# A heads stage whose next head begins in the tail of the current one, with the gate projected ahead of the values

## The chip, the cores and the metric

One Trainium2 chip, one core of it. The metric is device time in microseconds of the whole program. The program runs several stages one behind the other; the change touches one of them, the stage of heads, which takes the stretch from about 125 to 1003 us of a profiled execution of 5142.65 us.

## What is computed

The stage computes, for each of 8 heads of 128 channels, a bidirectional gated linear recurrence over 512 tokens that starts from the state of 256 context tokens, and one block of a depthwise convolution with 31 taps. Cut to what matters here:

```python
f = lb + (1 - lb) * sigmoid(z);  log_f = log(f);  k = (1 - lb) * sigmoid(-z)   # per direction
S_t = diag(f_t) S_{t-1} + k_t outer v_t;   o_t = S_t^T q_t                    # forward and backward
q = silu(x @ w_q);  v = x @ w_i;  gate = silu(x @ w_g)
hg = rms_norm(o_f + o_b) * silu(gate)
u = a * sigmoid(g)                                                            # conv_glu
u = depthwise_conv(u, 31 taps) + bias
```

Everything is float32, the matrix products too. Each head needs nine projections: `ca` and `cg` (the two inputs of the convolution), the gate logits of the two directions, the same two for the context, `q`, the values `v` for the 512 tokens, the values for the context, and `gate`.

## The kernel before

`phase_heads` runs one loop over the 8 heads on each engine, with the engines tied by counting semaphores. Nothing orders the work but the order in which each engine's program is written.

- **SyncE** loads the seven weight tiles of a head (512 KB each) into a ring of 7 slots, each as soon as its slot is free.
- **TensorE** calls `fill(n, head)` for the nine projections, n = 0 to 8. Fills 6, 7 and 8 of a head open the body of that head. Then come nine levels of a divide-and-conquer: for the first seven, two score products each (L734, on `qk`), and behind level 1 to 6 one of the fills 0 to 5 of the *next* head. Then the rest of the scores (L744, L749, L755, L761, L772), the output product with the values (L779, L781) and the sum of squares (L785).
- **VectorE** makes the logarithms and `k` from what ScalarE left (L890 to L895), and then runs the levels: three taps of the convolution, two running sums (L941, L950), the product `qk` (L966), and two masked copies out of PSUM (`to_blocks`, L928). After level 8 come the last taps, `ksum` (L973), `full` (L976, L977) and the last masked copy. The body ends with the scaling by the reciprocal root (L982) and the product with the gate (L985).
- **ScalarE** copies the projections out of PSUM (`evacuate`), computes the exponentials that each level needs (`grow`, L840), and has a tail: copies of the scores (L850 to L861), copy and square of the output (L864, L865), then `gates` of the next head (three copies, Abs, Exp, Ln: L809 to L818), the reciprocal root of this head (L869, L871) and `queries` of the next head (Silu).

A "tap" is one `scalar_tensor_tensor` on 128x512, 31 for each head. Of a fill, TensorE can start only when the bank it writes was copied out; a fill n below 4 waits for all nine copies of the head before. "Tail" below is the stretch from the start of the last masked copy of a head (level 8 is over) to the first running sum of the next head.

Of the kernel before, what the change touches and what calls it, by code (L numbers as in the profile page):

```python
# [12 lines left out]
ALU = mybir.AluOpType  # L13
# [585 lines left out]
def phase_heads(nc, io, mem):  # L599
# [20 lines left out]
    LINKS_DVE = 2 + 2 * LEVELS  # L620
    with Phase(nc, "hd") as ph:

        w = ph.stream(RING, [(1, AHEAD, [0, 1, 4, 4, 5]), (HEADS - 1, F, [1, 2, 3, 4, 7, 7, 8]),
                             (1, F - AHEAD, [1, 2])])
# [36 lines left out]
        @block.sync  # L661
        def _(sp):
            def load(t, head):
                load_tile(sp, w, *place(t, head), io["w_head"][head, t])
# [12 lines left out]
        def _(pe):  # L677
# [20 lines left out]
            def fill(n, head):  # L698
# [3 lines left out]
                if n < 4:  # L702
                    last = project(n, head, mem.xmT, bank)
                elif n == 4:
                    project(2, head, mem.cmT, bank[:, 0:C])
                    last = project(3, head, mem.cmT, bank[:, C:2 * C])
                elif n == 5:
                    last = project(4, head, mem.xmT, bank)
                elif n == 6:
                    last = tokens(5, head, mem.xmT, TB, bank)  # L710
                elif n == 7:
                    last = tokens(5, head, mem.cmT, CB, bank)
                else:
                    last = project(6, head, mem.xmT, bank)
                last.then_inc(w.filled, 1)

            def body(i, more):
# [59 lines left out]
                pe.wait_ge(proj_out, START + i * F + 8)  # L777
# [16 lines left out]
        def _(act):  # L794
# [10 lines left out]
            def gates(head):  # L805
# [10 lines left out]
                nc.scalar.activation(pre[:], pre[:], ACT.Exp, scale=-1.0).then_inc(act_seq, 1)  # L816
                act.wait_ge(act_seq, START + head * 2 + 2)
                nc.scalar.activation(pre[:], pre[:], ACT.Ln, bias=mem.c("one")).then_inc(ln_ready, 1)  # L818

            def queries(head):  # L820
                evacuate(5, head, q[:], B[1], ACT.Silu)

            def body(i, more):
                act.wait_ge(lk_ready, START + i + 1)
                nc.scalar.activation(k[:], k[:], ACT.Exp).then_inc(k_ready, 1)
                act.wait_ge(o_filled, START + i)
                evacuate(6, i, v[:, 0:TB, :], B[2].rearrange("p (b n) -> p b n", b=TB))
                evacuate(7, i, v[:, TB:TB + CB, :], B[3][:, 0:C].rearrange("p (b n) -> p b n", b=CB))
                act.wait_ge(head_done, START + i)
                evacuate(8, i, gate[:], B[0], ACT.Silu)  # L830
                for level in range(LEVELS):
# [34 lines left out]
                if more:  # L866
                    gates(i + 1)
# [4 lines left out]
                if more:  # L872
                    queries(i + 1)

            conv_inputs(0)
            gates(0)
            queries(0)
# [5 lines left out]
        def _(dve):  # L883
# [3 lines left out]
            with dve.Fori(0, HEADS) as i:  # L887
                seq.body(i, LINKS_DVE)
                dve.wait_ge(ln_ready, START + i + 1)
# [3 lines left out]
                nc.vector.memset(suf[:], 0.0)  # L893
# [3 lines left out]

                dve.wait_ge(proj_out, START + i * F + 2)
                dve.wait_ge(tapped, START + i * TAPS)
                nc.vector.tensor_tensor(out=upad[:, TAPS // 2:TAPS // 2 + T], in0=ca[:], in1=cg[:],  # L900
                                        op=ALU.mult).then_inc(conv_read, 1)
                weights = mem.p("dw").rearrange("p (b k) -> p b k", b=DB)[:, i, :]
                acc = mem.convT[:, i, :]
                left = list(range(TAPS))

                def taps(n):

                    for _ in range(min(n, len(left))):
                        tap = left.pop(0)
                        if tap == 0:  # L910
                            dve.wait_ge(conv_read, START + i + 1)
                            ins = nc.vector.tensor_scalar(acc, upad[:, 0:T], weights[:, 0:1],
                                                          mem.p("conv_b")[:, bass.ds(i, 1)], ALU.mult, ALU.add)
                        else:
                            dve.wait_ge(tapped, START + i * TAPS + tap)
                            ins = nc.vector.scalar_tensor_tensor(out=acc, in0=upad[:, tap:tap + T],
                                                                 scalar=weights[:, tap:tap + 1], in1=acc,
                                                                 op0=ALU.mult, op1=ALU.add)
                        ins.then_inc(tapped, 1)
# [52 lines left out]
                taps(TAPS)  # L972
# [6 lines left out]
                to_blocks(N_MASKS - 1)  # L979

# [5 lines left out]
            seq.end(HEADS)  # L986
# [2128 lines left out]
```

## Time and profile before

| what | value |
|---|---|
| median of three runs | 5145.26 us (5143.11 to 5145.98) |
| profiled execution, its own time | 5142.65 us |
| its span | 5140.9 us |
| mean granted clock of TensorE | 0.949 of full speed |
| busy over the span: TensorE, VectorE, ScalarE | 89%, 54%, 34% |
| stage of heads | about 125 to 1003 us |

A time stamp in the trace is microseconds from the start of the span. The shares are averages over stages that are limited by different engines; for this change only the stretch of the heads counts. A granted clock of 1.0 is 2.4 GHz, of 0.5 it is 1.2 GHz.

### The profile page before, as it was taken

Reading aid. Unit: us, or ns where it says so; the run is one execution under the profiler, and the core shown is the slowest. Engines: PE = TensorE matmul, PEld = TensorE weight load, DVE = VectorE, ACT = ScalarE, POOL = GpSimd, SP = SyncE. Lnnn points to the kernel's source line nnn. Section 1 sums busy time; section 2 is a strip of 40 time slices with the busy share of each in tenths; the row PEclk is TensorE's granted clock in tenths of the full one; section 3 lists DMA queues with packets and bytes.
Section 4 is the critical chain, followed back from the end, with each engine's and each line's share of the span. In section 5 each row is a group of like instructions: output and inputs, shape, how many; then the busy total and the mean of one; then the engine's idle time right before and its main releaser. Section 6 shows DMA issues by size and latency. Waiting matters only on the chain. (4 is left out here: it accounts for less than half of the span.)

```text
span 5140.9 us, 60695 instructions
## 1 busy us (share of the span) xinstructions
PE 4583.3 (89%) x21819; PEld 3657.5 (71%) x21819; DVE 2766.2 (54%) x5003; ACT 1741.5 (34%) x2490; POOL 412.8 (8%) x308
## 2 busy tenths in 40 slices
PE   7988888588899856699999999698999999999998
PEld 5555555344587425699999999576778877678787
DVE  0557775522334599788888887434343333444332
ACT  0243333223432103333333332336432233452322
POOL 0000000000000160122222222000000000000000
PEclk8999999799999979899999999899999999999999
DMA  6100110000122102678777875221222321113222
GB/s 259 58 29 29 37 37 21 21 28 16 41 94 93 49 19 123 228 274 282 272 274 276 280 274 200 70 70 44 73 92 96 95 86 62 50 62 98 89 95 84
DMA packets 195766, 575.47 MB, mean 112 GB/s; under 512 B 17312, under 2 KB 66720, under 8 KB 194336
## 3 DMA queue, kind: packets, MB, share of 16 engines
q1 hardware_dynamic: 157888, 433.77, 24.4%
q0 software_dynamic: 36864, 134.23, 7.7%
q10 hardware_dynamic: 864, 5.45, 0.3%
q8 instruction: 95, 1.56, 0.1%
q14 instruction: 55, 0.45, 0.0%
HBM read 546.13 MB, written 27.26 MB: 112 GB/s over the span
## 5 line engine op out<-in xcount | busy, mean ns | idle before, releaser
L402 DVE TENSOR_TENSOR tile_rest<-tile_raw,tile_up 128x1024 fp32r<-128x1024 f32 (+2 forms) x288 | 338.7, 1181 | 781.0 <-ACT tile_up L393 780.9
L410 PE MATMUL layer_psum<-hn_up,tile_up 128*128 128x512 f32 x1344 | 534.7, 398 | 21.2 <-DVE hn_rest L497 21.2
L411 PE MATMUL layer_psum<-hn_up,tile_rest 128*128 128x512 f32 x1344 | 527.0, 392 | 0.0
L412 PE MATMUL layer_psum<-hn_rest,tile_up 128*128 128x512 f32 x1344 | 526.7, 392 | 0.0
L393 ACT ACTIVATE tile_up<-tile_raw 128x1024 fp32r<-128x1024 f32 (+2 forms) x288 | 291.4, 1017 | 368.8 <-PE layer_psum L412 368.4
L687 PE MATMUL hd_psum<-xmT,hd_w 128*128 128x512 f32 x768 | 341.5, 599 | 15.7 <-DMA hd_w<-in_w_head 15.7
L1896 PE MATMUL ex_psum<-ex_t_up,ex_u_up 128*128 128x384 f32 x1024 | 344.2, 336 | 10.7 <-ACT ex_prod L1970 6.3
L1914 PE MATMUL ex_psum<-ex_prod_up,ex_v_up 128*128 128x384 f32 x1024 | 342.8, 335 | 3.8 <-DVE xT L2036 3.8
L1897 PE MATMUL ex_psum<-ex_t_up,ex_u_rest 128*128 128x384 f32 x1024 | 343.9, 336 | 0.0
L1898 PE MATMUL ex_psum<-ex_t_rest,ex_u_up 128*128 128x384 f32 x1024 | 343.7, 336 | 0.0
L1915 PE MATMUL ex_psum<-ex_prod_up,ex_v_rest 128*128 128x384 f32 x1024 | 342.6, 335 | 0.0
L1916 PE MATMUL ex_psum<-ex_prod_rest,ex_v_up 128*128 128x384 f32 x1024 | 342.6, 335 | 0.0
L410 PEld LDWEIGHTS layer_psum<-hn_up,tile_up 128*128 128x128 f32 x1344 | 255.2, 190 | 81.7 <-issue 29.7
L411 PEld LDWEIGHTS layer_psum<-hn_up,tile_rest 128*128 128x128 f32 x1344 | 255.1, 190 | 53.9 <-issue 1.9
L412 PEld LDWEIGHTS layer_psum<-hn_rest,tile_up 128*128 128x128 f32 x1344 | 254.7, 189 | 53.9
L687 PEld LDWEIGHTS hd_psum<-xmT,hd_w 128*128 128x128 f32 x768 | 144.6, 193 | 180.6 <-issue 180.6
L1962 ACT ACTIVATE ex_v_up<-tT 128x1024 fp32r<-128x1024 f32 x128 | 128.7, 1052 | 305.4 <-PE ex_psum L1916 301.7
L734 PE MATMUL hd_psum<-hd_qk 128*128 128x128 f32 x896 | 139.0, 320 | 91.3 <-DVE hd_qk L966 91.3
L734 PEld LDWEIGHTS hd_psum<-hd_qk 128*128 128x128 f32 x896 | 133.4, 232 | 115.2 <-issue 68.1
L1896 PEld LDWEIGHTS ex_psum<-ex_t_up,ex_u_up 128*128 128x128 f32 x1024 | 193.7, 189 | 11.4 <-issue 11.4
L1914 PEld LDWEIGHTS ex_psum<-ex_prod_up,ex_v_up 128*128 128x128 f32 x1024 | 192.7, 188 | 4.2 <-DVE xT L2036 4.2
L2036 DVE SCALAR_TENSOR_TENSOR xT<-ex_psum,modulation,xT 128x384 f32<-128x384 f32 x256 | 156.8, 612 | 71.7 <-PE ex_psum L1916 71.7
(415 smaller groups left out, 9532.8 us busy)
## 6 DMA issues: line engine op xcount, KB each, us to landing
ex_u<-in_peer_u SPq DMA_DIRECT2D x128, 512.0 KB, 6.7
tT<-in_peer_v SPq DMA_DIRECT2D x128, 512.0 KB, 7.2
tile_raw<-in_w_gu SPq DMA_DIRECT2D x88, 512.0 KB, 3.3
hd_w<-in_w_head SPq DMA_DIRECT2D x56, 512.0 KB, 3.9
mod_w<-in_w_ada SPq DMA_DIRECT2D x48, 512.0 KB, 4.9
mg_w_raw<-in_w_merge SPq DMA_DIRECT2D x48, 512.0 KB, 3.3
expert_table<-et_rows SPq DMA_DIRECT2D x6, 4096.0 KB, 11.7
ex_rows<-expert_table SPq DMA_DIRECT2D x64, 384.0 KB, 7.9
```

What stands on the lines that cost most here:

```text
L393: self.nc.scalar.activation(self.up[:, n % self.SLOTS, 0:blocks, :], self.raw[n % self.RAWS][:, 0:blocks, :], ACT.Copy).then_inc(self.up_r ...
L402: self.nc.vector.tensor_tensor(out=self.rest[:, n % self.SLOTS, 0:blocks, :], in0=self.raw[n % self.RAWS][:, 0:blocks, :], in1=self.up[:, ...
L410: self.nc.tensor.matmul(dst, w_up, up, start=first, stop=False)
L411: self.nc.tensor.matmul(dst, w_rest, up, start=False, stop=False)
L412: return self.nc.tensor.matmul(dst, w_up, rest, start=False, stop=last)
L687: last = nc.tensor.matmul(dst, weights[:, d, :], rhs[:, d, :], start=d == 0, stop=d == DB - 1)
L1896: nc.tensor.matmul(dst, u_up[par, t][:, d, :], t_up[:, d, :], start=d == 0, stop=False)
L1897: nc.tensor.matmul(dst, u_rest[par, t][:, d, :], t_up[:, d, :], start=False, stop=False)
L1898: last = nc.tensor.matmul(dst, u_up[par, t][:, d, :], t_rest[:, d, :], start=False, stop=d == DB - 1)
L1914: nc.tensor.matmul(dst, v_up[par, t][:, m, :], prod_up[par, t][:], start=first, stop=False)
L1915: nc.tensor.matmul(dst, v_rest[par, t][:, m, :], prod_up[par, t][:], start=False, stop=False)
L1916: last = nc.tensor.matmul(dst, v_up[par, t][:, m, :], prod_rest[par, t][:], start=False, stop=final)
```

## The change

Six edits, all in the stage of heads.

1. VectorE: a new function `start(head)` holds the opening of a head (clearing `suf`, the product `upad`, taps 0 to 13, the logarithms and `k`). It is called for head 0 ahead of the loop, and for head i+1 in the body of head i, between the last masked copy and the scaling by the reciprocal root.
2. VectorE: the levels then do 2 taps each instead of 3; level 8 does the one that is left. None stands behind level 8.
3. The body of the last head is written out behind the loop on VectorE, as it already was on TensorE and ScalarE.
4. ScalarE: `gates` is split. `decays` (three copies, Abs, Exp) stands ahead of the copy of the output, `log_decays` (Ln) where `gates` stood.
5. ScalarE: the copy of `q` moves out of the tail into the opening of the body, behind the exponential of `k`; `gate` follows it; the two copies of the values move behind `grow` of level 1.
6. TensorE: fill 6 is now the gate, fills 7 and 8 the values; the weight tiles are loaded in that order too. The output product waits for all nine copies.

The diff, cut to its core:

```diff
+    EARLY_TAPS = 14
-        w = ph.stream(RING, [(1, AHEAD, [0, 1, 4, 4, 5]), (HEADS - 1, F, [1, 2, 3, 4, 7, 7, 8]),
-                             (1, F - AHEAD, [1, 2])])
+        w = ph.stream(RING, [(1, AHEAD, [0, 1, 4, 4, 5]), (HEADS - 1, F, [0, 2, 3, 4, 7, 7, 8]),
+                             (1, F - AHEAD, [0, 2])])
...
                 elif n == 6:
-                    last = tokens(5, head, mem.xmT, TB, bank)
+                    last = project(5, head, mem.xmT, bank)
                 elif n == 7:
-                    last = tokens(5, head, mem.cmT, CB, bank)
+                    last = tokens(6, head, mem.xmT, TB, bank)
                 else:
-                    last = project(6, head, mem.xmT, bank)
+                    last = tokens(6, head, mem.cmT, CB, bank)
...
             def body(i, more):
                 act.wait_ge(lk_ready, START + i + 1)
                 nc.scalar.activation(k[:], k[:], ACT.Exp).then_inc(k_ready, 1)
-                act.wait_ge(o_filled, START + i)
-                evacuate(6, i, v[:, 0:TB, :], B[2].rearrange("p (b n) -> p b n", b=TB))
-                evacuate(7, i, v[:, TB:TB + CB, :], B[3][:, 0:C].rearrange("p (b n) -> p b n", b=CB))
+                evacuate(5, i, q[:], B[1], ACT.Silu)
                 act.wait_ge(head_done, START + i)
-                evacuate(8, i, gate[:], B[0], ACT.Silu)
+                evacuate(6, i, gate[:], B[2], ACT.Silu)
...
+                    if level == 1:
+                        act.wait_ge(o_filled, START + i)
+                        evacuate(7, i, v[:, 0:TB, :], B[3].rearrange("p (b n) -> p b n", b=TB))
+                        evacuate(8, i, v[:, TB:TB + CB, :], B[0][:, 0:C].rearrange("p (b n) -> p b n", b=CB))
...
+                if more:
+                    decays(i + 1)
                 act.wait_ge(masked, START + i * N_MASKS + N_MASKS)
                 act.wait_ge(o_filled, START + i + 1)
...
                 if more:
-                    gates(i + 1)
+                    log_decays(i + 1)
...
-                if more:
-                    queries(i + 1)
...
+            def start(head):
+
+                nc.vector.memset(suf[:], 0.0)
+                dve.wait_ge(proj_out, START + head * F + 2)
+                dve.wait_ge(tapped, START + head * TAPS)
+                nc.vector.tensor_tensor(out=upad[:, TAPS // 2:TAPS // 2 + T], in0=ca[:], in1=cg[:],
+                                        op=ALU.mult).then_inc(conv_read, 1)
+                taps(head, 0, EARLY_TAPS)
+                dve.wait_ge(ln_ready, START + head + 1)
                 seq(nc.vector.scalar_tensor_tensor(out=pre[:], in0=k[:], scalar=0.0, in1=pre[:], op0=ALU.min,
                                                    op1=ALU.subtract))
                 nc.vector.tensor_sub(k[:], pre[:], k[:]).then_inc(lk_ready, 1)
...
-                    taps(3)
+                    taps(i, EARLY_TAPS + 2 * level, EARLY_TAPS + 2 * level + 2)
...
                 to_blocks(N_MASKS - 1)
+                if more:
+                    start(i + 1)
 
                 dve.wait_ge(rstd_ready, START + i + 1)
```

VectorE at the end of a head, before (`hd_o` is the scaled output, `hgT` the head's result); what stands behind the last row here is the head of the loop, with L890 first:

```order
L977 TENSOR_TENSOR hd_full<-hd_full,hd_q 128x2x512
L925 REGISTER_ALU
L928 COPY_PREDICATED hd_sx<-masks,hd_psum 128x4x128
L982 SCALAR_TENSOR_TENSOR hd_o<-hd_o,params,hd_orstd 128x512
```

and the same place of the change, where 14 taps write `convT` between the masked copy and `hd_o`:

```order
L979 TENSOR_TENSOR hd_full<-hd_full,hd_q 128x2x512
L927 REGISTER_ALU
L930 COPY_PREDICATED hd_sx<-masks,hd_psum 128x4x128
L908 MEMSET hd_suf 128x1536
L909 ISA
L910 ISA
L911 TENSOR_TENSOR hd_upad<-hd_conv_a,hd_conv_g 128x512
...
L915 SCALAR_TENSOR_TENSOR hd_pre<-hd_k,hd_pre 128x1536
L221 REGISTER_ALU
L917 TENSOR_TENSOR hd_k<-hd_pre,hd_k 128x1536
L919 TENSOR_SCALAR hd_pre<-hd_pre 128x1536
L986 SCALAR_TENSOR_TENSOR hd_o<-hd_o,params,hd_orstd 128x512
```

The whole opening of the next head has moved ahead of `hd_o` and of the wait for `hd_orstd` in front of it.

ScalarE in the tail, before (`hd_sc` are scores of the context, `hd_osq` the squared output, `hd_pre` the logarithms being made):

```order
L861 ACTIVATE hd_sc<-hd_psum 128x512
L862 ISA
L864 ACTIVATE hd_o<-hd_psum 128x512
L865 ACTIVATE hd_osq<-hd_psum 128x512
...
L814 ACTIVATE hd_pre<-hd_k 128x1536
L815 ISA
L816 ACTIVATE hd_pre<-hd_pre 128x1536
L817 REGISTER_ALU
L818 ACT_TABLE_LOAD
L818 ACTIVATE hd_pre<-hd_pre,consts 128x1536
L869 ACTIVATE hd_orstd<-hd_psum,consts 128x512
```

and of the change:

```order
L863 ACTIVATE hd_sc<-hd_psum 128x512
L808 ISA
L809 ISA
...
L815 ACTIVATE hd_pre<-hd_k 128x1536
L816 ISA
L817 ACTIVATE hd_pre<-hd_pre 128x1536
L866 ISA
L868 ACTIVATE hd_o<-hd_psum 128x512
L869 ACTIVATE hd_osq<-hd_psum 128x512
L820 REGISTER_ALU
L821 ACT_TABLE_LOAD
L821 ACTIVATE hd_pre<-hd_pre,consts 128x1536
L873 ACTIVATE hd_orstd<-hd_psum,consts 128x512
```

The three copies, Abs and Exp now stand ahead of the copy of the output; Ln still stands between the square and the reciprocal root. At the head of ScalarE's loop the change has:

```order
L825 ACT_TABLE_LOAD
L825 ACTIVATE hd_k<-hd_k 128x1536
L798 ISA
L799 ACT_TABLE_LOAD
L799 ACTIVATE hd_q<-hd_psum 128x512
L827 REGISTER_ALU
L798 REGISTER_ALU
L799 ACTIVATE hd_gate<-hd_psum 128x512
L830 ISA
L838 ACT_TABLE_LOAD
L838 ACTIVATE hd_grow<-hd_suf 128x256
```

Before, the two copies of the values and a table load of their own for `hd_gate` stood in the place of `hd_q` and its load.

## Rows read from the trace of the kernel before

**Rows 1.** Stretch, length, busy PE PEld DVE ACT POOL, PE's granted clock, DMA share, GB/s.

```profile
497.00:512.00 15.00, 6.39 (x32) 6.21 (x33) 12.73 (x25) 5.40 (x13) 0.00 (x0) 0.69 0.00 0
512.00:565.00 53.00, 50.91 (x194) 30.32 (x192) 47.02 (x92) 13.23 (x30) 0.00 (x0) 0.99 0.13 46
```

**Rows 2.** Who waited for whom, 280 to 1003 us: us in total, times, longest.

```profile
DVE hd_o L982 <- ACT hd_orstd L871: 182.3, 8, 23.9
```

**Rows 3.** VectorE's timeline, one tail: start, length, instruction, idle before and releaser.

```profile
463.30 0.73 DVE L928 COPY_PREDICATED hd_sx<-masks,hd_psum 128x512 f32<-128x512 uint8 x1 [0.30 <-PE hd_psum L744]
487.50 0.75 DVE L982 SCALAR_TENSOR_TENSOR hd_o<-hd_o,params,hd_orstd 128x512 f32<-128x512 f32 x1 [23.47 <-ACT hd_orstd L871]
...
489.07 1.75 DVE L890 SCALAR_TENSOR_TENSOR hd_pre<-hd_k,hd_pre 128x1536 f32<-128x1536 f32 x1
...
492.88 1.34 DVE L893 MEMSET hd_suf<- 128x1536 f32 x1 [0.27 <-issue]
...
499.75 1.03 DVE L941 TENSOR_TENSOR hd_suf<-hd_suf,hd_pre 128x384 f32<-128x384 f32 x2 [1.47 <-ACT hd_grow L840]
```

**Rows 4.** VectorE's timeline, levels of the head that follows.

```profile
510.40 2.53 DVE L916 SCALAR_TENSOR_TENSOR convT<-hd_upad,params,convT 128x512 f32 x3
512.85 1.02 DVE L941 TENSOR_TENSOR hd_suf<-hd_suf,hd_pre 128x384 f32<-128x384 f32 x2
...
565.50 0.68 DVE L973 TENSOR_TENSOR hd_ksum<-hd_k 128x512 f32<-128x512 f32 x1
```

**Rows 5.** ScalarE's timeline, the same tail.

```profile
476.48 0.60 ACT L864 ACTIVATE hd_o<-hd_psum 128x512 f32<-128x512 f32 x1 [5.57 <-PE hd_psum L781]
...
477.45 1.58 ACT L798 ACTIVATE hd_k<-hd_psum 128x512 f32<-128x512 f32 x3
...
482.08 1.28 ACT L818 ACT_TABLE_LOAD   x1
483.37 1.57 ACT L818 ACTIVATE hd_pre<-hd_pre,consts 128x1536 f32<-128x1536 f32 x1
...
492.65 1.48 ACT L825 ACTIVATE hd_k<-hd_k 128x1536 f32<-128x1536 f32 x1 [1.97 <-DVE hd_k L892]
...
498.27 0.43 ACT L840 ACTIVATE hd_grow<-hd_suf 128x256 f32<-128x256 f32 x1
```

**Rows 6.** TensorE's timeline, the same tail.

```profile
461.40 1.66 PE L744 MATMUL hd_psum<-hd_q,hd_ksum 128*128 128x128 f32 x8 [3.42 <-DVE hd_ksum L973]
...
466.68 3.60 PE L772 MATMUL hd_psum<-hd_full 128*128 128x512 f32 x8
...
478.57 7.31 PE L694 MATMUL hd_psum<-hd_w,xmT 128*128 128x128 f32 x64
...
489.29 7.03 PE L687 MATMUL hd_psum<-xmT,hd_w 128*128 128x512 f32 x16
```

**Rows 7.** TensorE's timeline, levels 1 and up of the head that follows.

```profile
509.04 3.25 PE L734 MATMUL hd_psum<-hd_qk 128*128 128x128 f32 x16 [2.29 <-DVE hd_qk L966]
...
519.44 1.95 PE L734 MATMUL hd_psum<-hd_qk 128*128 128x128 f32 x16
521.23 7.03 PE L687 MATMUL hd_psum<-xmT,hd_w 128*128 128x512 f32 x16
528.09 1.95 PE L734 MATMUL hd_psum<-hd_qk 128*128 128x128 f32 x16
```

**Rows 8.** VectorE's waits for TensorE at levels 6 and 7 of that head.

```profile
546.70 0.73 DVE L928 COPY_PREDICATED hd_sx<-masks,hd_psum 128x512 f32<-128x512 uint8 x1 [1.15 <-PE hd_psum L734]
...
555.39 0.73 DVE L928 COPY_PREDICATED hd_sx<-masks,hd_psum 128x512 f32<-128x512 uint8 x1 [1.31 <-PE hd_psum L734]
```

**Rows 9.** Head 0: TensorE's first fill 6; VectorE's scaling of heads 0 and 6.

```profile
165.70 7.31 PE L694 MATMUL hd_psum<-hd_w,xmT 128*128 128x128 f32 x64
...
279.27 0.75 DVE L982 SCALAR_TENSOR_TENSOR hd_o<-hd_o,params,hd_orstd 128x512 f32<-128x512 f32 x1 [23.49 <-ACT hd_orstd L871]
...
903.92 0.75 DVE L982 SCALAR_TENSOR_TENSOR hd_o<-hd_o,params,hd_orstd 128x512 f32<-128x512 f32 x1 [23.47 <-ACT hd_orstd L871]
```

More of the change, by code:

```diff
@@ L663, in load @@
             def load(t, head):
-                load_tile(sp, w, *place(t, head), io["w_head"][head, t])
+                load_tile(sp, w, *place(t, head), io["w_head"][head, (0, 1, 2, 3, 4, 6, 5)[t]])
             for t in range(5):
@@ L803, in conv_inputs, with decays @@
                 evacuate(1, head, cg[:], B[1], ACT.Sigmoid)
-            def gates(head):
+            def decays(head):
                 act.wait_ge(qk_ready, START + head * (LEVELS + 2))
@@ L871, in body @@
                 nc.scalar.activation(orstd[:], orstd[:], ACT.Exp, scale=-0.5).then_inc(rstd_ready, 1)
-                if more:
-                    queries(i + 1)
             conv_inputs(0)
-            gates(0)
-            queries(0)
+            decays(0)
+            log_decays(0)
             with act.Fori(0, HEADS - 1) as i:
@@ L886, in _, with taps @@
             seq = Order(dve, dve_seq)
-            with dve.Fori(0, HEADS) as i:
-                seq.body(i, LINKS_DVE)
-                dve.wait_ge(ln_ready, START + i + 1)
+            def taps(head, first, past):
+                weights = mem.p("dw").rearrange("p (b k) -> p b k", b=DB)[:, head, :]
+                acc = mem.convT[:, head, :]
+                for tap in range(first, min(past, TAPS)):
+                    if tap == 0:
+                        dve.wait_ge(conv_read, START + head + 1)
+                        bias = mem.p("conv_b")[:, bass.ds(head, 1)]
+                        ins = nc.vector.tensor_scalar(acc, upad[:, 0:T], weights[:, 0:1], bias, ALU.mult, ALU.add)
+                    else:
+                        dve.wait_ge(tapped, START + head * TAPS + tap)
+                        ins = nc.vector.scalar_tensor_tensor(out=acc, in0=upad[:, tap:tap + T],
+                                                             scalar=weights[:, tap:tap + 1], in1=acc,
+                                                             op0=ALU.mult, op1=ALU.add)
+                    ins.then_inc(tapped, 1)
+            def start(head):
[6 more added lines that the diff above has]
+                dve.wait_ge(ln_ready, START + head + 1)
                 seq(nc.vector.scalar_tensor_tensor(out=pre[:], in0=k[:], scalar=0.0, in1=pre[:], op0=ALU.min,
@@ L892, in _, with body @@
                 nc.vector.tensor_sub(k[:], pre[:], k[:]).then_inc(lk_ready, 1)
-                nc.vector.memset(suf[:], 0.0)
                 nc.vector.tensor_scalar_max(pre[:], pre[:], LN_TINY).then_inc(logs_ready, 1)
[L898 to L919, printed above, removed]
+            def body(i, more):
                 def to_blocks(n):
@@ L971, in _ @@
                         to_blocks(2 * level - 1)
-                taps(TAPS)
+                taps(i, EARLY_TAPS + 2 * LEVELS, TAPS)
                 nc.vector.tensor_tensor(out=ksum[:], in0=k[:, 0, 0:T], in1=k[:, 1, 0:T],
@@ L985, in _ @@
                 nc.vector.tensor_tensor(out=mem.hgT[:, i, :], in0=o[:], in1=gate[:], op=ALU.mult).then_inc(head_done, 1)
-            seq.end(HEADS)
+            seq.body(0, 1)
+            start(0)
+            seq.end(1)
+            with dve.Fori(0, HEADS - 1) as i:
+                seq.body(i, LINKS_DVE)
+                body(i, True)
+            seq.end(HEADS - 1)
+            seq.body(0, LINKS_DVE - 1)
+            body(HEADS - 1, False)
+            seq.end(1)
             dve.wait_ge(head_done, START + HEADS)
```

5 lines of the change are left out of this document (2 added, 3 removed).

## The prediction, made before the change was run

> **What bounds the kernel now.** I first read who waited for whom in the stage of heads. One wait stands out: VectorE waits 182.3 us over 8 heads for `hd_orstd` before it scales the output, 23 us in each head [rows 2]. Then I read the timelines of the three engines through one such tail. VectorE ends level 8 with the masked copy at 463.30 and does nothing until 487.50 [rows 3]. ScalarE meanwhile copies the output at 476.48, then does the next head's three copies, Abs, Exp and Ln (477.45 to 484.9), and only then the reciprocal root [rows 5]. After the wait VectorE opens the next head: logarithms at 489.07, clearing at 492.88, first running sum at 499.75 [rows 3]. All this is work of the next head that needs nothing of this head's output.
>
> Next I looked at what TensorE does, for it has a limit of its own. It ends a head's last fill at 458, waits 3.42 for `ksum`, finishes the output sum at 478.57 and projects fills 6 to 8 from there [rows 6]. From level 1 on it repeats one pattern: a score pair and a fill, 519.44 to 528.09, 8.65 us [rows 7]. VectorE's level takes 7.28, of which three taps are 510.40 to 512.85, 2.45 us, 0.82 a tap [rows 4]. So TensorE is already the slower of the two in the levels, and VectorE waits for it 1.15 us at level 6 and 1.31 at level 7 [rows 8]. In levels 1 to 8 TensorE is busy 50.9 of 53 us [rows 1]. What VectorE gains beyond these waits is therefore not all gained by the head. A head now takes (903.92 - 279.27) / 6 = 104.1 us [rows 9].
>
> **The change part by part.** I follow one steady head and call F the start of fill 6, 478.57 [rows 6].
>
> *ScalarE's tail.* The three copies, Abs and Exp take 482.08 - 477.45 = 4.63 [rows 5] and move ahead of the output copy. There ScalarE idles 5.57 [rows 5], so they cost nothing, with 0.9 to spare. If that cover were gone, each microsecond of lateness would delay the output copy and with it L785 and F. The table load and Ln, and with them the reciprocal root, come earlier by 4.5: Ln starts at 483.37 - 4.5 = 478.85 (F+0.3), `ln_ready` is at F+1.85, and the root is ready at F+4.4 instead of F+8.93 [rows 3, 5].
>
> *VectorE's tail.* The opening now follows the masked copy. From 492.88 to 499.75, less the wait of 1.47, a clearing, L895, `upad` and three taps take 5.40 [rows 3]. Eleven more taps are 9.0, the copy and the issue gap 0.9: together 15.3 from the start of the masked copy. That copy starts 1 us behind L744, and `ln_ready` is 17.3 us behind L744 (below, 15.47 + 1.85). So 14 taps, 11.5 us a head, lie in idle time, and VectorE still waits 2 us for Ln. Then L915 and L917 take 492.88 - 489.07 - 0.27 = 3.54 [rows 3], so `lk_ready` comes at F+5.4. L919 (0.81), the scaling and the product with the gate (489.07 - 487.50 = 1.57 [rows 3]) end by F+8. Queued behind them are two taps and the first running sum.
>
> *ScalarE's opening.* Behind the root the loop's table load ends at F+5.7, a little after `lk_ready`. Then come Exp of `k`, a load, `q`, `gate` and a load. Before, the stretch from Exp of `k` to the first `grow` was 498.27 - 492.65 = 5.62 [rows 5], with the copies of the values and a short wait in it; now it has `q` instead of these, 5.3. I take `grow` at F+11.0, and VectorE's first running sum 1.48 later [rows 3, 5], at F+12.45 instead of F+21.18: 8.7 us earlier.
>
> *TensorE.* Fills 6 to 8 are the same work in another order: 10.72 for the values (489.29 - 478.57) [rows 6] and 8.65 - 1.79 = 6.86 for the gate [rows 7], 17.58 in all, ending at F+17.6. The gate is ready at F+7, before it is asked for (F+8). Level 0's `qk` is ready at F+15.9, so the 7 us idle ahead of level 0 are gone. Level 0's scores end at F+19.4. Level 1's `qk` comes at 509.04 - 8.7 - 0.82 (one tap less), F+20.95, so TensorE waits 1.5 there [rows 7]. Then six patterns of 8.65 follow, 51.9, and the last fill ends at F+72.85. VectorE's `ksum` is ready earlier: before, it started 65.75 after the first running sum (565.50 - 499.75) [rows 3, 4]; less 13 taps (10.7) and the waits of 2.46 [rows 8] it starts at F+65.1. So VectorE is ahead and waits inside the levels, some 7 us in all. From L744 to the next F it is 478.57 - 461.40 = 17.17 now [rows 6], of which the first 5.28 (461.40 to 466.68) hold 4,096 columns at the lower clock, right behind 3.42 idle. 2,048 columns take 1.79 in [rows 7] at the full clock, so 3.58 without the idle, and L744 to F is 15.47. Period: 72.85 + 15.47 = **88.3 us**, 15.8 less than 104.1.
>
> *The late copies of the values.* They wait on ScalarE for fill 8 (F+17.6), behind `grow` of level 1; `grow` of level 2 is queued behind them. TensorE needs the ninth copy for fill 0 at F+22.7, VectorE needs `grow` of level 2 at F+24. Both have 4 us to spare. *The tiles* are asked for in the new order almost a head ahead, and the DMA share is 0.13 [rows 1]: nothing. *The written-out body* adds no work.
>
> *Sum.* Head 0: F is 165.70 [rows 9], its scaling falls at 165.70 + 88.3 + 6.3 = 260.3 instead of 279.27: 19.0. Six periods of 15.8: 94.8. The last head has no fills, so there VectorE's own path counts: from scaling to first running sum 6.3 less (12.25 [rows 3] to 5.95), and 13 taps less, 10.7: 17.0. Together 130.8 us. The profiled execution took 5142.65, so 5011.9; the median of the runs is 2.6 higher, and I forecast **5014**.
>
> *A rule against it.* ScalarE's path to level 0 has five table loads behind the output copy. In this trace Ln starts 1.29 us after its load does and the load is 1.28 long, with no gap ahead of it either [rows 5]: a load costs 1.28. The Trainium skill, page "ScalarE: Activation LUTs", section "What ACT_TABLE_LOAD costs", puts a drain of some 1.38 us on top of each switch. By that page level 0 would be some 6.9 us later, TensorE's wait at level 1 as much longer, and the time an estimated 48 us more, 5062. The rows have no such gap, and I go by the rows.
>
> **The rivals.**
>
> *TensorE keeps falling to the lower clock (5050).* In 497 to 512 the granted clock is 0.69, behind 7 us of idle, and a score stretch takes 3.25 instead of 1.95 [rows 1, 7]. If the remaining waits (1.5 at level 1, some 2 in the tail) had the same effect, levels 0 and 1 would cost 3.4 more and L744 to F 1.7 more: 5.1 in each of 7 heads, 36 us. Against it: behind the 0.7 and 1.2 of the present tail, fills run at full speed (10.72 for the values [rows 6]).
>
> *VectorE's own path sets the period (4965).* If TensorE's waits vanished from the levels, the head would follow VectorE, 7 us less, 49 us in all. Against it stand the 8.65 of [rows 7], which nothing in the change shortens.
>
> *The tail work lands on the path (no change).* If the early three copies waited for something late, ScalarE would reach the output copy late, and the 14 taps would push the scaling. It takes a lateness of 15.8 us a head to eat the gain; I see at most 0.9 us missing.
>
> *Slower: fills at half clock.* A fill is 6.86 at 2.4 GHz and 13.7 at 1.2. The gain of 15.8 is gone once 2.3 of a head's nine fills run at the lower level; with four of nine there it is 7 x (27.4 - 15.8) = 81 us slower, 5226. It would need short gaps to bring the clock down. The stretch with most fills has 0.99 [rows 1].
>
> **How the numbers follow.** The forecast as walked has 0.66, its own range 5000 to 5030: without TensorE's wait at level 1 it is 10 us lower, with 2 us a head more it is 14 higher. The lower clock (5050) has 0.17, the drain 0.02, a smaller unforeseen wait between these and 5100 has 0.04, VectorE's path 0.04, no change 0.03, slower 0.04. The range 4998 to 5052 takes in the first two. What a measurement of this kernel can tell from no change is 0.2%, 10 us: faster 0.93, same 0.03, slower 0.04.
>
> **What would show it.** Right: VectorE's wait for the reciprocal root is gone, 2 us before L915 in its place; the scalings of heads 0 and 6 are 530 us apart; VectorE waits for TensorE's scores from level 4 on, and TensorE's patterns stay at 8.65; the granted clock in the heads is above 0.97; `qk` of level 0 finds TensorE still in fill 8. Wrong: TensorE idle ahead of level 0, the output copy later than 5.6 us behind the last score copy, score stretches of 3 us in the loop, or taps slower than 0.82 while ScalarE works on `k`.

## The result, and the profile of the changed kernel

The changed kernel takes a median of **5011.89 us** (5008.62 to 5017.14, four runs); the kernel before took 5145.62 on the same chip (5143.11 to 5149.23, four runs). The ratio is 0.9741, with a 95% interval of 0.9724 to 0.9757: 133.7 us less. The forecast was 5014.

The page of the changed kernel opens with its span, and its first group gives busy time, share and instructions of each engine. VectorE, with 2767.6 us of busy time, does what it did; what shrank are the span and TensorE's busy time (4583.3 before), which is shorter where the clock is up.

```profile
span 5012.3 us, 60591 instructions
...
PE 4546.6 (91%) x21819; PEld 3631.0 (72%) x21819; DVE 2767.6 (55%) x5003; ACT 1730.1 (35%) x2481; POOL 412.9 (8%) x308
```

The view of waits, for 250 to 890 us (us in total, times, longest), answers to [rows 2]: the 182.3 us that VectorE waited for the reciprocal root are gone in all heads but the last, where no next head is there to be opened. In their place VectorE now waits for TensorE's scores, at most 2.2 us at a time.

```profile
DVE hd_sx L930 <- PE hd_psum L735: 36.6, 18, 2.2
...
DVE hd_o L986 <- ACT hd_orstd L875: 17.5, 1, 17.5
```

VectorE's timeline (start, length, instruction, idle before and releaser) answers to [rows 3, 4, 8, 9]. 261.25 and 791.38 are the scalings of heads 0 and 6, 869.15 that of the last head. From 417.54 on it is one tail: masked copy, clearing, 13 taps in one row, then the logarithms at 433.63 with a wait of 0.74 for Ln, and the first running sum at 444.14. The rows at 479.88 to 497.23 are waits for the scores of levels 4 to 6, which VectorE copies in its own levels 5 to 7, as [rows 8] counts them.

```profile
261.25 0.74 DVE L986 SCALAR_TENSOR_TENSOR hd_o<-hd_o,params,hd_orstd 128x512 f32<-128x512 f32 x1
...
417.54 0.73 DVE L930 COPY_PREDICATED hd_sx<-masks,hd_psum 128x512 f32<-128x512 uint8 x1 [1.25 <-PE hd_psum L745]
...
418.52 1.34 DVE L908 MEMSET hd_suf<- 128x1536 f32 x1 [0.25 <-issue]
...
421.39 11.50 DVE L901 SCALAR_TENSOR_TENSOR convT<-hd_upad,params,convT 128x512 f32 x13
433.63 1.76 DVE L915 SCALAR_TENSOR_TENSOR hd_pre<-hd_k,hd_pre 128x1536 f32<-128x1536 f32 x1 [0.74 <-ACT hd_pre L821]
...
444.14 1.03 DVE L943 TENSOR_TENSOR hd_suf<-hd_suf,hd_pre 128x384 f32<-128x384 f32 x2 [2.96 <-ACT hd_grow L838]
...
479.88 0.73 DVE L930 COPY_PREDICATED hd_sx<-masks,hd_psum 128x512 f32<-128x512 uint8 x1 [1.85 <-PE hd_psum L735]
...
488.53 0.73 DVE L930 COPY_PREDICATED hd_sx<-masks,hd_psum 128x512 f32<-128x512 uint8 x1 [2.04 <-PE hd_psum L735]
...
497.23 0.73 DVE L930 COPY_PREDICATED hd_sx<-masks,hd_psum 128x512 f32<-128x512 uint8 x1 [2.19 <-PE hd_psum L735]
...
791.38 0.75 DVE L986 SCALAR_TENSOR_TENSOR hd_o<-hd_o,params,hd_orstd 128x512 f32<-128x512 f32 x1
...
869.15 0.75 DVE L986 SCALAR_TENSOR_TENSOR hd_o<-hd_o,params,hd_orstd 128x512 f32<-128x512 f32 x1 [17.47 <-ACT hd_orstd L875]
```

ScalarE's timeline of the same tail answers to [rows 5]. The idle time ahead of the output copy is 1.14 us instead of 5.57, for three copies, Abs and Exp now stand ahead of it. The table load at 430.73 follows it, and Ln 1.29 behind the load's start.

```profile
429.62 0.60 ACT L868 ACTIVATE hd_o<-hd_psum 128x512 f32<-128x512 f32 x1 [1.14 <-PE hd_psum L782]
...
430.73 1.28 ACT L821 ACT_TABLE_LOAD   x1
432.02 1.57 ACT L821 ACTIVATE hd_pre<-hd_pre,consts 128x1536 f32<-128x1536 f32 x1
```

TensorE's timeline answers to [rows 6, 7]. Fill 6 starts at 431.72, level 0's scores at 449.31 right behind fill 8, level 1's at 452.53 behind a wait of 1.27. From there to the next L745, at 504.59, nothing waits.

```profile
416.24 1.05 PE L745 MATMUL hd_psum<-hd_q,hd_ksum 128*128 128x128 f32 x8
...
430.76 1.13 PE L786 MATMUL hd_psum<-hd_osq,consts 128*128 128x512 f32 x2 [1.23 <-ACT hd_osq L869]
431.72 7.03 PE L688 MATMUL hd_psum<-xmT,hd_w 128*128 128x512 f32 x16
...
449.31 1.95 PE L735 MATMUL hd_psum<-hd_qk 128*128 128x128 f32 x16
452.53 2.05 PE L735 MATMUL hd_psum<-hd_qk 128*128 128x128 f32 x16 [1.27 <-DVE hd_qk L968]
454.41 7.03 PE L688 MATMUL hd_psum<-xmT,hd_w 128*128 128x512 f32 x16
...
504.59 1.05 PE L745 MATMUL hd_psum<-hd_q,hd_ksum 128*128 128x128 f32 x8
```

The windows of the changed kernel (columns as in [rows 1]): TensorE is busy for 40.00 of 40 us in the levels, VectorE for 32.23, and the granted clock is 1.00 there and 0.97 over the stage.

```profile
464.00:504.00 40.00, 40.00 (x158) 24.75 (x157) 32.23 (x66) 11.90 (x26) 0.00 (x0) 1.00 0.12 42
...
125.00:870.00 745.00, 692.89 (x3055) 448.50 (x3053) 573.37 (x1023) 310.64 (x560) 0.00 (x0) 0.97 0.11 38
```

The period of a head is (791.38 - 261.25) / 6 = **88.36 us**, 15.75 less than the 104.11 of before.

### The profile page after: what moved, and what is told of

Its sections match the earlier page's. It is cut to its first block and busy times, and to the rows that moved or that the text cites. A ratio compares the mean times of both kernels' runs of the same rounds, so it can differ in the third digit from the quotient of the medians.

```text
span 5012.3 us, 60591 instructions
## 1 busy us (share of the span) xinstructions
PE 4546.6 (91%) x21819; PEld 3631.0 (72%) x21819; DVE 2767.6 (55%) x5003; ACT 1730.1 (35%) x2481; POOL 412.9 (8%) x308
## 5 line engine op out<-in xcount | busy, mean ns | idle before, releaser
L1911 PEld LDWEIGHTS ex_psum<-ex_t_up,ex_u_rest 128*128 128x128 f32 x1024 | 193.5, 189 | 0.0
L1912 PEld LDWEIGHTS ex_psum<-ex_t_rest,ex_u_up 128*128 128x128 f32 x1024 | 193.3, 189 | 0.0
```

What stands on the lines that cost most here:

```text
L1911: nc.tensor.matmul(dst, u_rest[par, t][:, d, :], t_up[:, d, :], start=False, stop=False)
L1912: last = nc.tensor.matmul(dst, u_up[par, t][:, d, :], t_rest[:, d, :], start=False, stop=d == DB - 1)
```

## The experiments

**Theory A**, the one of the prediction: TensorE's own chain sets the head. It gains what its first idle stretches lose, ahead of level 0, at level 1 and ahead of L744; whatever VectorE is relieved of beyond that is hidden. The time at which `qk` of level 1 is ready is what each part of the change acts on. **Theory B**, the rival: VectorE's work sets the head, so each tap that leaves the levels is worth its 0.88 us (11.50 / 13; the recorded expectations price it at 0.82), and the order of the fills is secondary. Ratios are to the kernel before on the same chip. The period is the spacing of VectorE's scalings of heads 0 to 6 (of the mean, where they alternate). The diffs are against the changed kernel unless said otherwise.

### 1. taps_in_levels: ten of the 14 early taps back in the levels

```diff
-    EARLY_TAPS = 14
+    EARLY_TAPS = 4
...
-    taps(i, EARLY_TAPS + 2 * level, EARLY_TAPS + 2 * level + 2)
+    taps(i, EARLY_TAPS + 3 * level, EARLY_TAPS + 3 * level + 3)
```

> The changed kernel with 4 taps in the opening instead of 14 and 3 taps in each level, as before, instead of 2. Theory A, TensorE's chain sets the head: VectorE's level grows from 6.4 to 7.2 us and stays below TensorE's 8.65, so only the one tap more ahead of level 1 counts, 0.8 us a head, perhaps 1 more at the end where VectorE's ksum comes close: period 89 to 90.5, 5018 to 5028, ratio 0.975 to 0.977. Theory B, what counts is VectorE work moved into its idle tail: ten taps put back are 8.2 us in each of 7 heads, about 58 us: 5070, ratio 0.985.

Measured: 5032.31 us, ratio 0.9776 (0.9763 to 0.9789). The period is 90.4 instead of 88.36, 2.1 more where B wants 8.8, so A holds for the loop. But the time lies 4 us above A's range. One part I had left out of the expectation: in the last head TensorE has no fills, VectorE's own path sets it, and it took 84.72 from scaling to scaling instead of 77.77. The other part is TensorE's timeline at level 1, here of two heads one behind the other:

```profile
368.18 2.05 PE L735 MATMUL hd_psum<-hd_qk 128*128 128x128 f32 x16 [2.18 <-DVE hd_qk L968]
370.07 7.03 PE L688 MATMUL hd_psum<-xmT,hd_w 128*128 128x512 f32 x16
...
457.75 2.51 PE L735 MATMUL hd_psum<-hd_qk 128*128 128x128 f32 x16 [2.17 <-DVE hd_qk L968]
460.06 8.30 PE L688 MATMUL hd_psum<-xmT,hd_w 128*128 128x512 f32 x16
```

The wait is 0.9 longer, for one tap more stands ahead of level 1's `qk`. In every second head the clock falls behind it (granted clock 0.89 in 449 to 464 us), and scores and fill together take 1.7 more. The periods alternate, 91.26 and 89.58. So 0.9 is the tap and 0.85 in the mean is the clock. Another 0.3 is lost at the end of the levels, where `ksum` now comes late: from the start of the last fill to L745 it is 7.10 instead of 6.87, and from L745 to L773 3.61 instead of 3.51. The sum over the loop, 12.4, and the last head, 7.0, make the 20.

### 2. taps_22_early: eight more taps ahead

```diff
-    EARLY_TAPS = 14
+    EARLY_TAPS = 22
...
-    taps(i, EARLY_TAPS + 2 * level, EARLY_TAPS + 2 * level + 2)
+    taps(i, EARLY_TAPS + level, EARLY_TAPS + level + 1)
```

> The changed kernel with 22 taps in the opening and one in each level. VectorE now waits 0.74 us for Ln behind 14 taps, so 8 taps more (6.8 us) make the opening about 6.1 us late, and logarithms, gate product and level 0 with it. Theory A: level 1's product would be 6.1 late less 0.8 to 1.6 for the taps that no longer stand ahead of it, so TensorE waits about 5 us more a head: period 93, 5045, ratio 0.980. Theory B: more work in the tail helps further or costs nothing: 5012 or below.

Measured: 5052.02 us, ratio 0.9814 (0.9800 to 0.9827). Period 95.5, 7.1 more, where I had expected 93; the last head is 73.0, 4.8 less. VectorE had 0.74 us to spare ahead of the logarithms (the row at 433.63), so nearly all of eight taps land on the path to level 0. TensorE's timeline, levels 0 and 1:

```profile
562.57 3.77 PE L735 MATMUL hd_psum<-hd_qk 128*128 128x128 f32 x16 [5.39 <-DVE hd_qk L968]
566.50 2.93 PE L735 MATMUL hd_psum<-hd_qk 128*128 128x128 f32 x16 [0.15 <-DVE hd_qk L968]
```

Fill 6 of that head starts at 539.43, so level 1 starts at F+27.07 where it was F+20.81: 6.26 later, plus 0.88 for the lower clock behind the wait. VectorE does less in each level, and it helps nothing. This is the clearest case against B.

The expectation had taken 0.8 to 1.6 off for taps that no longer stand ahead of level 1's product. One tap less does stand there, but this is taken back ahead of level 0, as VectorE's timeline shows:

```profile
558.34 0.75 DVE L901 SCALAR_TENSOR_TENSOR convT<-hd_upad,params,convT 128x512 f32 x1 [4.68 <-issue]
```

The one tap of level 0 could run at 553.6, behind the product with the gate, and starts only when the last `grow` has ended (557.84). The first running sum follows that `grow` by 1.17 instead of 0.11. So some 1.0 of the 7.1 is the lateness of one tap, not the length of eight. It is so in each head of the loop, but not in the last, whose body is written out: there the tap starts at once, at 840.24. The profile names no releaser, and the cause is not shown.

### 3. decays_behind_output: the copies, Abs and Exp back behind the output copy

```diff
-                if more:
-                    decays(i + 1)
                 act.wait_ge(masked, START + i * N_MASKS + N_MASKS)
                 ...
                 if more:
+                    decays(i + 1)
                     log_decays(i + 1)
```

> The changed kernel with the next head's three copies, Abs and Exp behind the copy and square of the output again, together with Ln. Theory A: Ln and the reciprocal root come 4.6 us later, and with them level 1's product; the wait of TensorE there grows from 1.3 to about 5.9: period 93, seven times 4.6 = 32 us, 5044, ratio 0.9803. Theory B: VectorE's idle time in the tail grows by 4.6, no VectorE work moves; same cost if VectorE sets the head, none if it has slack in the levels: 5012 to 5044.

Measured: 5044.57 us, ratio 0.9800 (0.9786 to 0.9813). Periods 92.86 in four heads and 94.50 in two, 5.1 more in the mean. TensorE's timeline:

```profile
438.55 7.03 PE L688 MATMUL hd_psum<-xmT,hd_w 128*128 128x512 f32 x16
...
459.02 2.05 PE L735 MATMUL hd_psum<-hd_qk 128*128 128x128 f32 x16 [2.73 <-DVE hd_qk L967]
463.85 3.15 PE L735 MATMUL hd_psum<-hd_qk 128*128 128x128 f32 x16 [2.78 <-DVE hd_qk L967]
```

Level 1 starts 463.85 - 438.55 = F+25.30, 4.5 later, which is the 4.63 that was moved. The rest, 0.6 in the mean, is the clock. In two of the six periods level 1's scores are slow, as in the row at 463.85, and that costs 1.6. In the other four the clock falls behind the wait at level 0, whose scores then take 3.4 to 3.7; that only shortens the wait at level 1 and costs nothing. The expectation met its median.

### 4. values_first: the gate behind the values again

The fills 6 to 8, the loads and the copies are in the old order; all else stays.

```diff
                 elif n == 6:
-                    last = project(5, head, mem.xmT, bank)
+                    last = tokens(5, head, mem.xmT, TB, bank)
                 elif n == 7:
-                    last = tokens(6, head, mem.xmT, TB, bank)
+                    last = tokens(5, head, mem.cmT, CB, bank)
                 else:
-                    last = tokens(6, head, mem.cmT, CB, bank)
+                    last = project(6, head, mem.xmT, bank)
```

> The changed kernel with the values projected ahead of the gate again (tile order, fills 6 to 8, and ScalarE's copies: values, then gate, ahead of level 0). Theory A: the gate is ready at the end of fill 8, F+17.8, then copy, table load and grow, so the first running sum is at F+21.2 as before the change, 8.7 us later, and TensorE waits 8.7 us more at level 1: period 97, 5073, ratio 0.986. Rival: the order costs nothing, since the gate is only needed for the product with the output of this head's end and VectorE has slack: 5012.

Measured: 5095.38 us, ratio 0.9896 (0.9881 to 0.9911), 22 us above the expectation. Period 98.97, 10.6 more, and the last head 87.39, 9.6 more. ScalarE's timeline, the copy of the gate, and TensorE's:

```profile
481.55 0.60 ACT L799 ACTIVATE hd_gate<-hd_psum 128x512 f32<-128x512 f32 x1 [6.48 <-PE hd_psum L688]
```

```profile
463.76 7.31 PE L695 MATMUL hd_psum<-hd_w,xmT 128*128 128x128 f32 x64
...
488.51 3.78 PE L735 MATMUL hd_psum<-hd_qk 128*128 128x128 f32 x16 [6.99 <-DVE hd_qk L967]
493.34 3.78 PE L735 MATMUL hd_psum<-hd_qk 128*128 128x128 f32 x16 [1.05 <-DVE hd_qk L967]
```

ScalarE is ready for the gate 6.48 us early and stands at it, with the first `grow` queued behind. Level 1 starts at F+29.58, 8.77 later than with the gate ahead; the rest, 1.8, is the clock of two score stretches, which the expectation had not counted. So of the parts that were taken out of the whole, the gate's place is the largest: without it the early opening stops at the copy of the gate. VectorE's opening as a whole was not taken out by itself, and neither was the later `q`.

### 5. opening_only and 6. gate_first_only: one part alone, on the kernel before

opening_only gives the kernel before VectorE's part alone (`start` in the tail, 14 early taps); gate_first_only gives it the new order of fills alone, with the loads and copies that go with it (cut to its first line):

```diff
                 elif n == 6:
-                    last = tokens(5, head, mem.xmT, TB, bank)
+                    last = project(5, head, mem.xmT, bank)
```

> The kernel before with VectorE's part of the change alone: opening of the next head and 14 taps in the tail, 2 taps a level; ScalarE's and TensorE's orders are those of before. Theory A: level 0 still starts at F+21.2, because the gate is copied last; level 1's product is 0.8 earlier, TensorE's waits decide: period 97, some 7 us a head less than 104.1, and 10.7 in the last head: 5080, ratio 0.987. Theory B (moved VectorE work is what counts, 16 us a head): 5015 to 5030, ratio 0.977.

> The kernel before with only the gate projected and copied ahead of the values (and the values copied behind the exponentials of level 1). Both theories: VectorE's path is the bound there; ScalarE's copies of the values leave the stretch ahead of level 0, about 1 us, so 1 us a head at most: 5137, ratio 0.998. Theory A says with it that this part is worth 8.7 us a head in the changed kernel and 1 in the old one.

opening_only measured 5097.15 us, ratio 0.9898 (0.9883 to 0.9913), period 98.95 where 97 was expected. This is the period of values_first (98.97), which has ScalarE's split and the later `q` besides. So these two are worth nothing in the loop while the gate comes late: the same wait for the gate takes up what they give. In the kernel before, too, the copy of the gate stands right behind fill 8, as ScalarE's timeline shows:

```profile
496.36 0.60 ACT L798 ACTIVATE hd_gate<-hd_psum 128x512 f32<-128x512 f32 x1 [0.17 <-PE hd_psum L687]
```

What opening_only gains is elsewhere, at L745, in TensorE's timeline:

```profile
545.67 1.05 PE L745 MATMUL hd_psum<-hd_q,hd_ksum 128*128 128x128 f32 x8
...
549.18 3.60 PE L773 MATMUL hd_psum<-hd_full 128*128 128x512 f32 x8
```

With 13 taps fewer in the levels `ksum` is early. The wait of 3.42 ahead of it [rows 6] is gone, and what follows takes 3.51 instead of 5.28. These two make 5.2, the whole of the gain.

gate_first_only measured 5118.75 us, ratio 0.9940 (0.9927 to 0.9954), period 102.44. I had expected 5137. The first running sum comes at F+20.27 instead of F+21.18, as the expectation has it. But F to L744 takes 86.9 in both kernels (the mean of two heads, for the kernel before): the 0.9 is lost again, for from the first running sum to `ksum` it is 65.8 in every head, where it was 65.8 and 64.1 by turns. The gain is elsewhere, ahead of L744's scores in TensorE's timeline:

```profile
651.60 1.15 PE L744 MATMUL hd_psum<-hd_q,hd_ksum 128*128 128x128 f32 x8 [3.42 <-DVE hd_ksum L974]
...
655.21 3.60 PE L772 MATMUL hd_psum<-hd_full 128*128 128x512 f32 x8
```

The idle time ahead of L744 is 3.42 as in [rows 6], but what follows takes 3.61 instead of 5.28: the clock stays up, in all seven heads. That is the 1.67 of a head.

The finding of values_first and these two: the two parts alone gain 5.15 and 1.67 a head, and the whole gains 15.75. The other 9 belong to neither alone. ScalarE's split alone, and the split together with the gate but without VectorE's opening, were not run; by the row at 496.36, where ScalarE already waits 0.17 for fill 8, the split alone could not start the first `grow` earlier.

### 7. half_fills: what VectorE's own path is

It leaves out half of the contraction, four of eight blocks, of fills 0 to 3 of heads 1 to 7, so its output is another.

```diff
-                        fill(level - 1, i + 1)
+                        fill(level - 1, i + 1, True)
```

> The changed kernel, leaving out half of the contraction of fills 0 to 3 of heads 1 to 7 (four of eight blocks), 3.43 us each, 13.7 a head; the output is another one. If TensorE's chain alone sets the head, the period falls by all 13.7 to 74.7: 4916, ratio 0.955. Theory A with VectorE's own path as the next bound: period 81.4 to 83, a little more where TensorE idles and its clock falls ahead of L745: 4963 to 4975, ratio 0.964 to 0.967. If TensorE isn't the bound: 5012.

Measured: 4955.58 us, ratio 0.9623 (0.9608 to 0.9638), period 80.48. TensorE's timeline in the levels:

```profile
434.15 2.05 PE L735 MATMUL hd_psum<-hd_qk 128*128 128x128 f32 x16 [0.98 <-DVE hd_qk L968]
436.04 3.60 PE L688 MATMUL hd_psum<-xmT,hd_w 128*128 128x512 f32 x8
...
471.79 1.15 PE L745 MATMUL hd_psum<-hd_q,hd_ksum 128*128 128x128 f32 x8 [0.85 <-DVE hd_ksum L975]
```

Of 13.7 us less work (4 x 3.43) the head becomes 7.9 shorter. Now TensorE waits 0.9 to 1.0 for `qk` at each of levels 2 to 5, and 0.85 for `ksum`. So the changed kernel is limited by TensorE in the levels, and with the levels on VectorE's path the head is 7.9 us shorter. The prediction had put the distance at 7. The period is 0.9 below the lowest that was expected: the clock stayed up ahead of L773 (471.79 to 475.40).

### 8. fills_in_gaps: pieces of fills where TensorE still waits

Half of fill 0 goes ahead of level 1's scores, the last block of fill 5 ahead of the output product, and the first block of fill 6 ahead of the sum of squares.

```diff
-                    if more and level > 0:
+                    if more and level == 0:
+                        fill(0, i + 1, 0, DB // 2)
+                    elif more and level == 1:
+                        fill(0, i + 1, DB // 2)
+                    elif more and level < 6:
                         fill(level - 1, i + 1)
+                    elif more:
+                        fill(5, i + 1, 0, DB - 1)
 ...
+                if more:
+                    fill(5, i + 1, DB - 1)
 ...
+                if more:
+                    fill(6, i + 1, 0, 1)
```

> The changed kernel with TensorE's three gaps of a head filled by pieces of fills: half of fill 0 ahead of level 1's scores (gap of 1.27), the last block of fill 5 ahead of the output product (0.76), the first block of fill 6 ahead of the mean (1.23, a block is 0.86). Theory A: 1.27 + 0.76 + 0.86 = 2.9 us a head less, 7 heads, 20 us: 4992, ratio 0.970, period 85.5. If something else sets the period: 5012 or more, and the gaps reappear in other places.

Measured: 4989.69 us, ratio 0.9694 (0.9681 to 0.9708), the fastest version that computes everything, period 85.31, 3.05 less (85.5 and 4992 were expected). TensorE's timeline:

```profile
420.79 1.13 PE L797 MATMUL hd_psum<-hd_osq,consts 128*128 128x512 f32 x2 [0.38 <-ACT hd_osq L881]
...
438.48 1.95 PE L736 MATMUL hd_psum<-hd_qk 128*128 128x128 f32 x16
440.27 3.60 PE L688 MATMUL hd_psum<-xmT,hd_w 128*128 128x512 f32 x8
443.70 1.95 PE L736 MATMUL hd_psum<-hd_qk 128*128 128x128 f32 x16
```

The waits of 1.27 at level 1, 0.76 at the output product and most of the 1.23 at the sum of squares are filled: 0.38 is left. They make 1.27 + 0.76 + 0.85 = 2.9 of the 3.05.

### 9. square_first and 10. taps_gaps: two more on top of number 8

square_first puts ScalarE's Square ahead of its copy of the output, to take the last 0.38. taps_gaps puts ten early taps back into the levels (as number 1) on top of number 8.

```diff
-                nc.scalar.activation(o[:], B[4], ACT.Copy).then_inc(score_out, 1)
                 nc.scalar.activation(osq[:], B[4], ACT.Square).then_inc(o_squared, 1)
+                nc.scalar.activation(o[:], B[4], ACT.Copy).then_inc(score_out, 1)
```

> The kernel with TensorE's gaps filled, and on ScalarE the square of the output ahead of its copy instead of behind it. TensorE waits 0.38 us for the square behind the block of fill 6. The square is ready 0.5 us earlier, so the 0.38 go: period 84.9 instead of 85.3, 3 us in all, 4987, ratio 0.9688 against 0.9694; at the edge of what can be told. If anything but TensorE's chain sets the head: no change, 4990.

> TensorE's gaps filled, and 4 taps in the opening, 3 in each level. With 14 early taps the step between these two was 20 us (ratio 0.9776 against 0.9741: 2.1 us a head, of which the clock behind a wait of 2.2 us at level 1 seems to be 0.8). Theory A: the wait at level 1 is covered now, but TensorE reaches ksum earlier than VectorE with three taps a level: VectorE's ksum decides, period about 87, 5002, ratio 0.972. Rival, the early taps are worth the 8.2 us they take: 85.3 + 8.2, 5047, ratio 0.980.

square_first measured 4992.75 us, ratio 0.9705 (0.9692 to 0.9719), no difference to number 8, the period 85.31 again instead of the 84.9 that was expected. The 0.38 is gone from its place and stands at level 2, for ScalarE's Ln still starts behind the second of the two. TensorE's timeline:

```profile
449.40 2.05 PE L736 MATMUL hd_psum<-hd_qk 128*128 128x128 f32 x16 [0.44 <-DVE hd_qk L980]
```

taps_gaps measured 5020.05 us, ratio 0.9758 (0.9745 to 0.9771), period 88.44, where I had expected some 87. TensorE's timeline:

```profile
459.07 2.05 PE L736 MATMUL hd_psum<-hd_qk 128*128 128x128 f32 x16 [1.75 <-DVE hd_qk L980]
...
502.87 1.15 PE L752 MATMUL hd_psum<-hd_q,hd_ksum 128*128 128x128 f32 x8 [1.09 <-DVE hd_ksum L987]
```

Here VectorE sets the head: `ksum` starts at 502.06, 72.07 behind the main part of fill 6 (429.99), and TensorE waits for it. From there 0.81 to L752 and 15.59 to the next fill 6 make 88.47. My 87 was 1.4 too short; at which step is not known. So ten early taps are worth 3.1 us a head once TensorE's gaps are closed, and 2.1 before. That is still far from the 8.8 of B.

## Why the prediction was right

**The period.** Forecast 88.3, measured 88.36. The steps, each by the rows of the changed kernel:

- F to level 0's scores: forecast 17.6, measured 449.31 - 431.72 = 17.59. `qk` of level 0 finds TensorE still in fill 8.
- Level 1: forecast F+20.95 behind a wait of 1.5, measured F+20.81 behind 1.27. decays_behind_output, taps_22_early and values_first moved this one time by 4.5, 6.3 and 8.8 and the period by 5.1, 7.1 and 10.6: the head follows it, plus 0.6 to 1.8 for the clock.
- Fills at full speed, to L745: forecast F+72.85, measured 504.59 - 431.72 = 72.87.
- L745 to the next F: forecast 15.47, measured 431.72 - 416.24 = 15.48. The 3.42 of idle are gone and with them the lower clock. The forecast said that the 4,096 columns in the 5.28 ran at the lower clock; they take 3.51 at the full one, so only a part of them did. The sum does not use this.

**VectorE's tail.** I gave it 2 us to spare ahead of Ln and it had 0.74. The 13 taps took 11.50, 0.88 apiece instead of 0.82, and the last masked copy starts 1.3 behind L745 instead of 1.0. Nothing hung on it, but taps_22_early shows how near the edge was. Taps slower than 0.82 while ScalarE works on `k` stood among the signs of being wrong. ScalarE is not the reason, as VectorE's timeline in a level shows:

```profile
447.49 0.74 DVE L901 SCALAR_TENSOR_TENSOR convT<-hd_upad,params,convT 128x512 f32 x1
448.38 0.75 DVE L901 SCALAR_TENSOR_TENSOR convT<-hd_upad,params,convT 128x512 f32 x1 [0.15 <-DVE convT L901]
449.05 1.02 DVE L943 TENSOR_TENSOR hd_suf<-hd_suf,hd_pre 128x384 f32<-128x384 f32 x2
```

Each tap waits for the tap ahead of it, whose sum it takes up, and starts 0.89 behind it; the running sum, which needs no tap, starts 0.67 behind the last. Three taps are 0.89 + 0.89 + 0.67 = 2.45, the 0.82 apiece of [rows 4], and 13 in one row are all but 0.89 apiece. The 13 are spaced alike where ScalarE works on `k` and where it idles ahead of 429.62. So a tap that is added to a row or taken from it counts 0.89, in the levels too, and 0.82 was the wrong price for it.

VectorE waits for the scores, as forecast, but begins one level later than forecast, in its level 5: 1.85, 2.04, 2.19 and then 1.25 behind L745, 7.3 a head where some 7 were forecast. half_fills gives nearly the same distance to VectorE's own path, 7.9.

**ScalarE's tail.** 1.14 to spare where 0.9 were forecast. First running sum F+12.42, forecast F+12.45.

**Head 0 and the last.** From the first weight tile asked for to the first scaling it was 161.62 and is 141.45: 20.2 less, where 19.0 was forecast. The last head, scaling to scaling, was 97.12 and is 869.15 - 791.38 = 77.77: 19.35 less, where 17.0 was forecast. From scaling to first running sum it gains 7.63 instead of 6.3, for this stretch was 13.60 there and not the 12.25 of a steady tail. From there to `ksum` it gains 12.29 instead of 10.7, the 13 taps at 0.89 and some more. Behind `ksum` it loses 0.6. Six periods of 15.75 make 94.5. Together 134.0, forecast 130.8; the medians differ by 133.7. The 3 us of difference to the forecast are these two ends. The spans of the two profiled executions differ by less, 128.6. But that of the kernel before lies 3.0 below its median and that of the changed kernel 2.2 above, which is nearly all of it: it is the spread between executions.

**The rivals.** The lower clock stayed away from the loop: its longest wait is 1.27, no score stretch behind it is slow, and the granted clock is 1.00 from 260 to 790 us. The 0.97 of the whole stage comes from the last head, where TensorE has no fills, waits 2.5 to 4.2 at levels 2 to 6, and its score stretches take 2.8 to 3.8; VectorE sets that head. taps_in_levels shows that the lower clock was near: with a wait of 2.17 it falls in every second head. VectorE's path is 7.9 below, not the bound. The table loads have no drain: Ln starts 1.29 behind its load's start (432.02 - 430.73), and the load is 1.28 long, as before. The Trainium skill, page "ScalarE: Activation LUTs", section "What ACT_TABLE_LOAD costs", adds some 1.38 us of drain to each switch; by that page level 0 would have come late. The row at 449.31 has no wait, and the measurement decides.

**What I did not see ahead**: how little the parts are worth apart. The forecast walked the whole path with all edits in it, and that was right, but a reader could take from it that each step carries its own saving. values_first, opening_only, gate_first_only and decays_behind_output show that the gate, the opening on VectorE and the split on ScalarE are three inputs of one meeting point, level 0's first `grow`, and the latest decides.

## What to carry to other kernels

Walk from a fixed instruction on the bounding engine (here fill 6) to the next instance of it, and write down at each meeting point which of the inputs comes last: an edit is worth what it takes from the latest, and edits of different inputs are worth their sum only together. How much work can go into the idle time of a tail is set by the next wait behind it: 14 taps fit with 0.74 us to spare, eight more cost 7.1 us a head. An edit can also gain where it was not aimed: opening_only gained nothing ahead of level 0 and 5.2 us a head at `ksum`. When an engine becomes the bound, look for its remaining small waits and put pieces of independent work there: here three such pieces gave some 22 us more (5011.89 and 4989.69, on two chips).

## What the runs showed of the hardware

TensorE's granted clock does not depend on the length of one wait alone. Behind 1.27 us at level 1 it never fell in the changed kernel's heads; behind 2.17 and 2.18 it fell in every second head (taps_in_levels). Behind 2.73 at level 0 it fell in some heads (scores of 3.39 to 3.68) and not in others (2.05), which then had slow scores at level 1 behind 2.78 (decays_behind_output). Behind 3.42 ahead of the scores it fell in each of seven heads of the kernel before (5.28 to L772) and in none of gate_first_only (3.61), though the wait is the same and the five patterns of scores and fill ahead of it have the same lengths. What differs is the first part of the head, where the clock had fallen at another moment; that the moment is the reason is argued, not shown. Behind 5.4 (taps_22_early) level 0's scores took 3.77 and the next 2.93, behind 7.0 (values_first) both took 3.78, instead of 1.95. The Trainium skill, page "TensorE: Matmul & The Clock Gate", section "HAM oscillation — how this bites in real kernels", tells of a loop in which the clock falls again in each turn behind its wait. The kernel before agrees (seven of seven heads); taps_in_levels, with every second turn, and gate_first_only, with none, do not: one and the same wait can have a slow stretch behind it or not.

On VectorE an instruction that waits for the one ahead of it costs more than its own length: 0.89 us from one tap to the next, 0.67 to an instruction that does not wait (447.49 to 449.05).
